# Short convolution's projection as wide products with the halves added at eviction, two of its products on GpSimd

## What is computed

```
def short_conv_mixer(h, w_in, conv_w, w_out):
    bcx = h @ w_in                          # 1024 -> 3 * 1024
    b_gate, c_gate, xv = jnp.split(bcx, 3, axis=-1)
    u = b_gate * xv
    y = conv_general_dilated(u, conv_w, padding=[(2, 0)], feature_group_count=d)
    return (c_gate * y) @ w_out
```

## Time and profile before

| | us |
|---|---|
| median of 3 runs (1105.52 to 1106.31) | 1105.63 |
| the profiled execution | 1105.78 |
| its span in the profile | 1104.0 |
| PE busy | 1099.4 |
| DVE busy | 831.6 |
| ACT busy | 615.5 |
| POOL busy | 36.2 |

### The profile page before, as it was taken

One profiled execution on the slowest core, in us unless ns is written; L12 is line 12 of the kernel. 1 busy time (PEld: TensorE's weight loads), 2 busy tenths in 40 slices (PEclk: granted clock), 3 DMA queues, 4 the chain that ended last, 5 costly groups with the idle time before them and its releaser, 6 DMA issues.

```text
span 1104.0 us, 18914 instructions
## 1 busy us (share of the span) xinstructions
PE 1099.4 (100%) x7382; PEld 990.4 (90%) x7382; DVE 831.6 (75%) x1281; ACT 615.5 (56%) x964; POOL 36.2 (3%) x53
## 2 busy tenths in 40 slices
PE   9999999999999999999999999999999999999998
PEld 9999888888888988889899998888888789888887
DVE  6977897775676887776669867777666879877753
ACT  6656555554545656555545455666444777656631
POOL 0030000000000000000010000000001110000000
PEclk9999999999999999999999999999999999999999
DMA  8544455555485555555645545555554325555551
GB/s 318 199 159 185 169 202 187 188 195 205 148 262 165 186 180 192 191 191 191 223 158 171 202 169 186 191 191 191 191 208 152 137 77 196 187 191 191 196 195 68
DMA packets 33209, 203.78 MB, mean 185 GB/s; under 512 B 3936, under 2 KB 7264, under 8 KB 9824
## 3 DMA queue, kind: packets, MB, share of 16 engines
q1 hardware_dynamic: 32160, 202.12, 52.3%
q10 hardware_dynamic: 960, 0.45, 0.2%
HBM read 200.33 MB, written 2.23 MB: 183 GB/s over the span
## 4 chain that ended last, share of the span: by engine, by line
PE 98%; DMA 1%; SPq 0%; ACT 0%; DVE 0%; issue 0%; POOL 0%; DVEq 0%; ACTq 0%
PE banks L440 46%; PE banks L453 24%; PE banks L416 6%; PE banks L419 6%; PE banks L422 6%; PE banks L493 3%; PE banks L476 1%; PE banks L482 1%; PE banks L479 1%; DMA raw_t<-w 1%; PE banks L1716 1%; PE banks L1702 0%; PE banks L528 0%; PE banks L863 0%; PE banks L506 0%; PE banks L871 0%
## 5 line engine op out<-in xcount | busy, mean ns | idle before, releaser
L347 DVE TENSOR_TENSOR lo_t<-raw_t,hi_t 128x1024 fp32r<-128x1024 f32 x364 | 439.3, 1218 | 12.9 <-ACT hi_t L341 11.7
L341 ACT ACTIVATE hi_t<-raw_t 128x1024 fp32r<-128x1024 f32 x364 | 376.2, 1050 | 105.3 <-PE banks L453 39.2
L440 PE MATMUL banks<-x,hi_t 128*128 128x512 f32 x1536 | 362.6, 391 | 0.0
L440 PEld LDWEIGHTS banks<-x,hi_t 128*128 128x128 f32 x1536 | 283.7, 188 | 56.3 <-issue 0.4
L453 PEld LDWEIGHTS banks<-x,lo_t 128*128 128x128 f32 x1536 | 193.5, 191 | 5.4
L453 PE MATMUL banks<-x,lo_t 128*128 128x256 f32 x1536 | 195.7, 283 | 0.0
L440 PE MATMUL banks<-f,hi_t 128*128 128x512 f32 x704 | 164.1, 390 | 0.0
L440 PEld LDWEIGHTS banks<-f,hi_t 128*128 128x128 f32 x704 | 130.6, 188 | 26.1
L597 DVE TENSOR_TENSOR scr<-banks,scr 128x512 f32<-128x512 f32 x88 | 60.4, 690 | 75.3 <-ACT scr L666 75.0
L453 PEld LDWEIGHTS banks<-f,lo_t 128*128 128x128 f32 x704 | 87.6, 192 | 1.9
L453 PE MATMUL banks<-f,lo_t 128*128 128x256 f32 x704 | 88.2, 283 | 0.0
(11 more groups left out here) (210 smaller groups left out, 1094.7 us busy)
## 6 DMA issues: line engine op xcount, KB each, us to landing
raw_t<-w SPq DMA_DIRECT2D x182, 1024.0 KB, 4.9
f<-shifts SPq DMA_DIRECT2D x16, 287.0 KB, 4.6
raw_t<-w SPq DMA_DIRECT2D x3, 512.0 KB, 9.7
h<-xT SPq DMA_DIRECT2D x4, 256.0 KB, 7.7
out<-h SPq DMA_DIRECT2D x8, 128.0 KB, 3.7
cst<-consts SPq DMA_DIRECT2D x1, 800.0 KB, 9.8
shifts<-scr SPq DMA_DIRECT2D x5, 144.0 KB, 3.7
raw_t<-w SPq DMA_DIRECT2D x2, 256.0 KB, 5.4
```

What stands on the lines that cost most here:

```text
L341: e.activation(hi_t[:, p % RING, :], raw_of(p), ACT.Copy).then_inc(s_hi, 1)
L347: e.tensor_tensor(lo_t[:, p % RING, :], raw_of(p), hi_t[:, p % RING, :].bitcast(F32), ALU.subtract).then_inc(s_lo, 1)
L440: m = e.matmul(halves(banks[:, to[j], :]), hi_t[:, slot, r * P:(r + 1) * P], parts[:, ks[j], :, :], start=ks[j] == 0 and not low_first, st ...
```

## The change

- The projection's products are issued with `broad_run`. Unit j writes B to the bank b and X to b + 1, with b = 0 or 2 by turns, and C to bank 4 or 6 by turns. For B and X the high products come first, for C the low ones.
- PE waits ahead of B and X of unit j, from j = 2 on, until DVE has added unit j - 2 (s_bx), and ahead of C until DVE has added that C (s_sc1). The output product waits for s_bx of all eight units.
- ACT copies the second halves out: 512 columns for B and X, 256 for C.
- DVE adds: 512 columns for B and X together (sx_r), 256 for C.
- sb = B x rb2 moves to POOL. The factor on C, once C x rbc, becomes a factor on the convolution's result, yr = y x rbc, on POOL too.
- In DVE's order for a unit, the low split stands between the add and u; the splits behind the gate come later by the count of tiles.

```diff
-SHORT_BANKS = (2, 3, 4, 0, 1, 6)
+BX_BANKS = (0, 2)
+C_BANKS = (4, 6)
...
         def pe_short(e):
...
-            e.wait_ge(s_su, KD)
+            for j in range(KD):
+                if j == 1:
+                    pe_col_sums(e, 4)
+                if j == 2:
+                    pe_spread(e, 4)
+                if j >= 2:
+                    e.wait_ge(s_bx, j - 1)
+                b = BX_BANKS[j % 2]
+                broad_run(e, G_CI + 24 * j, [b] * KD + [b + 1] * KD, [*range(KD), *range(KD)], x2, KD - 1,
+                          (lambda k: x_of(4, k)) if j == 0 else None, LAST_LATE if j == 0 else None)
+                if j >= 2:
+                    e.wait_ge(s_sc1, j - 1)
+                broad_run(e, G_CI + 24 * j + 16, [C_BANKS[j % 2]] * KD, range(KD), x2, KD - 1, low_first=True)
+            e.wait_ge(s_bx, KD)
             e.wait_ge(s_sc1, KD - 1)
...
         def act_short(e):
...
+            for j in range(KD):
+                c = G_CI + max(24 * j + 16, 48)
+                hi_to(e, c)
+                e.wait_ge(s_tiles, upto(G_CI + 24 * j + 15))
+                if j >= 2:
+                    e.wait_ge(s_bx, j - 1)
+                e.activation(halves(sd_r[j % 2]), bx_pair(j, 1), ACT.Copy).then_inc(s_bxside, 1)
+                hi_to(e, c + 8)
+                e.wait_ge(s_su, j + 1)
+                if j >= 2:
+                    e.wait_ge(s_yr, j - 1)
+                e.activation(sy_r[j % 2], su_r[j % 2][:, 6:6 + T], ACT.Copy, scale=colv("w_c3", j)).then_inc(s_stap, 1)
+                e.wait_ge(s_tiles, upto(G_CI + 24 * j + 23))
+                if j >= 2:
+                    e.wait_ge(s_sc1, j - 1)
+                e.activation(cd_r[j % 2], banks[:, C_BANKS[j % 2], T:2 * T], ACT.Copy).then_inc(s_cside2, 1)
+                hi_to(e, G_CI + max(24 * j + 24, 48) + 3)
+                e.wait_ge(s_sgate, j + 1)
+                e.activation(fh[:, j, :], sc_r[j % 2], ACT.Copy).then_inc(s_fh, 1)
...
         def dve_short(e):
...
+            for j in range(KD):
+                c = G_CI + max(24 * j + 16, 48)
                 lo_to(e, c)
...
+                e.wait_ge(s_bxside, j + 1)
+                if j >= 2:
+                    e.wait_ge(s_sb, j - 1)
+                e.tensor_tensor(halves(sx_r[j % 2]), bx_pair(j, 0), halves(sd_r[j % 2]), ALU.add).then_inc(s_bx, 1)
+                lo_to(e, c + 3)
+                y, ub = sy_r[j % 2], su_r[j % 2]
+                e.wait_ge(s_sb, j + 1)
+                if j == 0:
+                    e.wait_ge(s_spad, 2)
+                e.tensor_tensor(ub[:, 8:US], sx_r[j % 2][:, T:2 * T], sb_r[j % 2], ALU.mult).then_inc(s_su, 1)
+                lo_to(e, c + 8)
+                e.wait_ge(s_stap, j + 1)
+                n = dv.mark(e.scalar_tensor_tensor(y, ub[:, 7:7 + T], colv("w_c3", 8 + j), y, ALU.mult, ALU.add))
+                e.wait_ge(dv.sem, n)
+                e.scalar_tensor_tensor(y, ub[:, 8:8 + T], colv("w_c3", 16 + j), y, ALU.mult, ALU.add).then_inc(s_sy, 1)
+                e.wait_ge(s_cside2, j + 1)
+                if j >= 2:
+                    e.wait_ge(s_fh, f_done(4, j - 2))
+                e.tensor_tensor(sc_r[j % 2], banks[:, C_BANKS[j % 2], 0:T], cd_r[j % 2], ALU.add).then_inc(s_sc1, 1)
+                e.wait_ge(s_sc1, j + 1)
+                e.wait_ge(s_yr, j + 1)
+                e.tensor_tensor(sc_r[j % 2], sc_r[j % 2], yr_r[j % 2], ALU.mult).then_inc(s_sgate, 1)
+                lo_to(e, G_CI + max(24 * j + 24, 48) + 11)
+                e.wait_ge(s_fh, f_done(4, j))
+                e.tensor_tensor(fl[:, j, :], sc_r[j % 2], fh[:, j, :].bitcast(F32), ALU.subtract).then_inc(s_fl, 1)
+                e.scalar_tensor_tensor(h[:, j, :], h[:, j, :], colv("fin_g", j), r1b, ALU.mult, ALU.mult).then_inc(s_res, 1)
...
         def pool_short(e):
...
+            e.wait_ge(s_rbc, RBC_AT[4] + 1)
+            for j in range(KD):
+                e.wait_ge(s_bx, j + 1)
+                if j >= 2:
+                    e.wait_ge(s_su, j - 1)
+                e.tensor_tensor(sb_r[j % 2], sx_r[j % 2][:, 0:T], rb2[:, :], ALU.mult).then_inc(s_sb, 1)
+                e.wait_ge(s_sy, j + 1)
+                if j >= 2:
+                    e.wait_ge(s_sgate, j - 1)
+                e.tensor_tensor(yr_r[j % 2], sy_r[j % 2], rbc[:, :], ALU.mult).then_inc(s_yr, 1)
```

More of the change, by code:

```diff
@@ L1499, in model_kernel @@
         S0 = 2 * US
-        sb_r = [scratch(S0 + n * T, T) for n in range(2)]
-        sc_r = [scratch(S0 + 2 * T + n * T, T) for n in range(2)]
-        sy_r = [scratch(S0 + 4 * T + n * T, T) for n in range(2)]
-        r1b = scratch(SCR - T, T)
-        s_spad, s_sc1, s_su, s_stap, s_sy, s_sgate, s_res = (
-            sem("spad"), sem("sc1"), sem("su"), sem("stap"), sem("sy"), sem("sgate"), sem("res"))
-        def pe_short(e):
[L1508 to L1522, removed]
-            e.wait_ge(s_su, KD)
@@ new lines, in model_kernel @@
+        sx_r = [scratch(S0 + n * 512, 512) for n in range(2)]
+        S1 = S0 + 1024
+        sd_r = [scratch(S1 + n * 512, 512) for n in range(2)]
+        S2 = S1 + 1024
+        sb_r, sc_r, sy_r, yr_r, cd_r = ([scratch(S2 + (2 * i + n) * T, T) for n in range(2)] for i in range(5))
+        assert S2 + 10 * T <= SCR - T
+        r1b = scratch(SCR - T, T)
+        s_spad, s_su, s_stap, s_sy, s_sgate, s_res = (
+            sem("spad"), sem("su"), sem("stap"), sem("sy"), sem("sgate"), sem("res"))
@@ new lines, in model_kernel, with bx_pair @@
+        s_bxside, s_cside2, s_bx, s_sb, s_yr, s_sc1 = (
+            sem("bxside"), sem("cside2"), sem("bx"), sem("sb"), sem("yr"), sem("sc1"))
+        def bx_pair(j, half):
+            b = BX_BANKS[j % 2]
+            return banks[:, b:b + 2, half * T:(half + 1) * T]
+        def pe_short(e):
+            for j in range(KD):
[5 more added lines that the diff above has]
+                    e.wait_ge(s_bx, j - 1)
+                b = BX_BANKS[j % 2]
+                broad_run(e, G_CI + 24 * j, [b] * KD + [b + 1] * KD, [*range(KD), *range(KD)], x2, KD - 1,
[4 more added lines that the diff above has]
+            e.wait_ge(s_bx, KD)
@@ L1526, in pe_short @@
             pe_out_rest(e, 4, G_CO, N_SHORT, range(KD))
-        def short_c(u):
-            return G_CI + max(24 * (u // 2) + (16, 24)[u % 2], 48)
         def act_short(e):
[L1533 to L1544, removed]
+            for j in range(KD):
[17 more added lines that the diff above has]
+                e.activation(fh[:, j, :], sc_r[j % 2], ACT.Copy).then_inc(s_fh, 1)
         def dve_short(e):
```

## The result

The changed kernel takes 1116.51 us (median; 1115.62 to 1117.30), the kernel before beside it 1105.97: a ratio of 1.0093, 95% interval 1.0081 to 1.0105. It is 10.5 us slower, where 5.6 were forecast; the time lies 2.5 us above the range. The profiled execution took 1115.99 with a span of 1114.2.

The account below looks back on a forecast made before the run. PE alone bounds the kernel before; after, DVE's handovers delay it. Parts: -2.5 (wide products) +2.2 +1.0 +0.3 +4.5 (PE's waits) = +5.5; +5.6 by the count, so 1111.2 us, range 1107.5 to 1114.0.

Parts of the forecast that it names:

- POOL's 0.61 us: Time of each product moved to POOL (sb, yr), taken from a 271-column addition of 0.64; slower products at 1.0: 7%.
- the slow clock: Rival: after the 4.5 us idle ahead of the output product PE runs slow, costing 1.7 to 2.5 us; 17%.
- start of DVE's chain: Short convolution: DVE's add of unit 0 starts at 578.60, 1.89 us behind the spread.
- The ceiling of the wide products: PE's short-convolution projection: 8.33 us a unit instead of 8.64, at most 2.5 us saved over 192 tiles.
- The wait at unit 2: PE idles 2.2 us at the head of unit 2 until DVE has added unit 0.
- 1.0 us wait forecast at C of unit 3: PE waits there for a low split that DVE does behind add 2, done at 594.24.
- DVE's unit: DVE's time per unit when behind PE: 8.41 us against PE's 8.33, so it never catches up.
- The exclusion of sb and the split: POOL's sb waits for DVE's low split to end, leaving DVE idle 0.61; the no-exclusion rival, 1107.6, had 9%.
- three handovers: DVE's waits in a unit for other engines ahead of u, first tap and gate: 1.9 us.
- the first rival: DVE keeps up, a unit costing at most 7.3 us: 1103.2 (3%), or 1105.4 with the wait at unit 2 (4%).
- The last wait: PE idles 4.5 us ahead of the output product, until DVE's add of unit 7 ends at 635.2.
- these two rivals: Slower POOL products, 1.0 us each: 1115.5, 7%; slow clock after PE's wait: 1113.3, 17%.

Follow-up runs that it names:

- e3: Changed kernel with sb and yr back on DVE and the low split between u and the first tap: 1107.61 us.
- e9: e5 with adds of units 0 and 1 and two low splits ahead of the spread wait, C of unit 3's split in unit 0: 1103.74 us.
- e2: Changed kernel with DVE adding unit 0 before it waits for the spread (transposes that give it the normalisation): 1115.66 us.
- e1: Changed kernel with odd units in banks 0 and 1, so the add of unit 6 empties the output product's first bank: 1109.94 us.
- e4: Changed kernel with the low split moved from ahead of u to behind it, sb and yr still on POOL: 1111.75 us.
- e8: Changed kernel with both of POOL's products turned into additions, so results differ: 1116.06 us, one run.
- e11: Changed kernel with yr turned into an addition of 271 columns on POOL, so results differ: 1115.75 us, one run.
- e10: Changed kernel with 18 products on ones into free bank 7 ahead of PE's wait before the output product: 1114.04 us.
- e5: Changed kernel with the edits of e1, e2 and e3 together: 1107.40 us.
- e6: Changed kernel with 36 products on ones into free bank 7 ahead of PE's wait before the output product: 1116.73 us.

## Why the prediction was wrong

The direction and the mechanism were right, and so were the places of the waits but for one. Two terms of the sum failed: POOL's 0.61 us, which was too small, and the slow clock, which the forecast put at nothing. The first, with a start of DVE's chain 0.18 us later than forecast, cost 2.3 us, the second another 2.3. The prediction expected 1111.4 for the profiled execution and it took 1115.99, 4.6 more, which is the two together; the median lies 0.5 above that execution.

- *The ceiling of the wide products:* right. 8.33 us a unit was taken from 32-tile runs of a feed-forward stage, and where PE waits for nothing a unit with runs of 16 and 8 takes 8.34 (e3). In the changed kernel it is 8.39 for unit 3 (587.78 to 596.17, from C to C). Over eight units the ceiling is 2.4 to 2.5 us; e9 keeps 1.7 of it in its trace.
- *The wait at unit 2:* forecast 2.2, measured 2.03. But counting it into the sum by parts was only bookkeeping: e2 shows that it was covered by DVE's chain. The clock fell to 0.52 behind it as well, and that slow stretch cost nothing for the same reason. It took the place of the 1.0 us wait forecast at C of unit 3: in e1 and e3, whose profiled executions have no slow stretch there, that wait is 1.45 and 0.93 us.
- *DVE's unit:* forecast 8.41, measured 8.72. The exclusion of sb and the split is confirmed by e4 (1.64 with it, 0.74 without), and the three handovers that the prediction called 1.9 us (its own terms give 0.61 + 0.67 + 0.48 = 1.76) are 1.79. The step that failed is "I take 0.61, the nearest row". The products take 0.73 to 0.74. That row was of 271 columns; the row of 257 columns, at 64.46, took 0.74 and was passed over. e8 and e11 show that neither operation nor width makes the difference. The 0.12 us enters the unit once with sb and, with handovers some hundredths longer, once with yr: 0.10 more from add to u, 0.20 more ahead of the gate. Seven units and a start 0.18 later make 2.3 us (add 7 at 636.79, forecast 634.46).
- *The busy work of a unit:* the first rival calls it 7.3 us. The prediction's own distances between starts add to 6.6 without the handovers. e3, with two operations more and no wait for another engine, takes 7.77, and that is short enough for DVE to catch up.
- *The last wait:* forecast 4.5, measured 4.45. Each C part of PE waits for a split of DVE's, so PE arrives late by the same amount as the add, and the wait stayed as foretold while both ends moved.
- *The slow clock:* given 17% as a rival of its own, at 1.7 to 2.5 us. It happened, and cost 2.1 to 2.5 us (e10), 2.3 in the trace. This is the greater failure of judgment. The forecast itself said PE would idle 4.5 us in one piece, longer than anything in the trace of before, and then summed as if the clock were sure to hold. The prediction had named the Trainium skill, "TensorE: Matmul & The Clock Gate", Part 1, for the rule that an idle array drops to half its clock; the trace agrees, with 0.50 in the window from 637 to 639.
- *The range:* each of these two rivals was priced and reached at most 1115.5 alone. They don't exclude each other: 1111.2 + 2.3 + 2.3 = 1115.8, against 1116.5 measured. The range stopped at 1114.0, between one and both.

Of the 10.5 us, the runs place some 2.3 in the clock (e10) and the rest in DVE's chain (e3 takes it and the clock away at once, 8.9 us, and leaves the wait at unit 2).

## What to carry to other kernels

Cost a move to another engine by the chain that it lengthens, not by the busy time that it frees: here two products of 0.42 us taken off DVE made its unit 0.95 us longer (0.51 with the split in the better place of e4), because both stand between an operation of DVE and the next. If the sum leaves PE idle in one piece, give the slow clock behind it a term of its own; behind 4.45 us it cost 2.3 here. Before an add of the two halves is set ahead of a wait, look at which unit's result empties the bank that the next product needs first; the order of two bank numbers was worth 6.6 us. When several rivals can hold at once, add their prices for the end of the range.

## What the runs showed of the hardware

- Short idling is enough for the clock. In the profiled runs it fell after waits of 4.43 to 4.48 us every time (changed kernel, e2, e8, e11), and after 2.19, 2.50 and 2.54 us in e2, e5 and e4; after waits of 1.45 and 1.63 us in e1 it did not. After the 2.03 us wait at unit 2 it fell in the changed kernel and in e4, e6, e10, e8 and e11, and did not in e1 and e3, though PE's program up to there differs in e1 by bank numbers alone and in e3 not at all. A wait of 2 us may or may not bring a slow stretch of some 3 us.
- One program does both. Of the ten runs of e3, four have a mean granted clock of 1.000 and six of 0.998; their medians, 1107.55 and 1107.64, are next to equal. So a slow stretch in this kernel can be free, while in e5, where nothing covers it, the runs without one are the two fastest.
- The fall can come behind the wait, with PE at work again: in the changed kernel the window from 577 to 579, mostly idle, reads 1.00, and that from 581 to 583, all busy, 0.52.
- A GpSimd operation issued behind a VectorE operation that reads two operands from SBUF waits for it: sb took 1.64 us behind the low split and 0.74 alone (changed kernel and e4).
- An addition of 128 x 271 on GpSimd took 0.64 us in one stage and 0.77 in another (e11), with nothing beside it that reads two operands from SBUF. The reason is open.
